# Mixture-of-experts turns: the ranks behind two fixed experts in order of size, in place of large and small in turn

## What is computed

```python
_, idx = lax.top_k(jnp.where(in_group, biased, -jnp.inf), TOP_K)      # TOP_K = 2 of 16
wts = jnp.take_along_axis(scores, idx, axis=-1)
wts = wts / wts.sum(-1, keepdims=True)
gates = jnp.einsum('tk,tke->te', wts, jax.nn.one_hot(idx, N_EXPERTS, dtype=F32)).astype(h.dtype)
y = jnp.zeros_like(x)
for e in range(N_EXPERTS):
    he = jax.nn.silu(x  wg[e]) * (x  wu[e])
    y = y + gates[:, e:e + 1] * (he  wd[e])
```

## Time and profile before

| | us |
|---|---|
| median of 3 runs | 1263.56 |
| the three runs | 1263.53, 1263.56, 1271.19 |
| the profiled execution, device time | 1273.05 |
| its span (first to last instruction) | 1270.9 |
| mean granted TensorE clock | 0.927 |
| TensorE busy (matmul) | 1055.2 (83%) |
| moved by DMA | 299.46 MB, mean 236 GB/s |

### The profile page before, as it was taken

The page is one execution under the profiler, slowest core; times in us unless marked ns, Lnnn a source line. Parts: engine busy times, 40 slices in busy tenths (PEclk is TensorE's granted clock), DMA queues, the critical chain, the costliest instruction groups (busy, mean ns, idle before and its releaser), DMA issues. The chain is left out here.

```text
span 1270.9 us, 14505 instructions
## 1 busy us (share of the span) xinstructions
PE 1055.2 (83%) x5804; PEld 615.9 (48%) x5804; DVE 346.0 (27%) x810; ACT 242.6 (19%) x542; POOL 141.3 (11%) x163
## 2 busy tenths in 40 slices
PE   4899997967898989677999867687785989998874
PEld 1344465833343434245887457577653433333333
DVE  0101125254010010123433266668236001010103
ACT  1200235121110111112333411121131101010112
POOL 1000000010000000001000056573000000000001
PEclk9999968978999999888999989899897999999988
DMA  9966840442689899992665310100060498989860
GB/s 375 428 273 265 310 180 7 143 188 103 268 367 415 371 405 388 386 426 95 225 258 207 144 46 1 67 1 1 23 242 2 166 431 344 429 348 428 342 291 33
DMA packets 22157, 299.46 MB, mean 236 GB/s; under 512 B 2560, under 2 KB 2688, under 8 KB 4032
## 3 DMA queue, kind: packets, MB, share of 16 engines
q1 hardware_dynamic: 20304, 291.34, 56.5%
q0 software_dynamic: 1776, 7.08, 1.5%
HBM read 295.27 MB, written 3.15 MB: 235 GB/s over the span
## 5 line engine op out<-in xcount | busy, mean ns | idle before, releaser
L496 PE MATMUL bank<-ring,arena 128*64 128x512 f32 x640 | 147.2, 612 | 23.0 <-DMA ring<-slots 14.3
L504 PE MATMUL bank<-ring,arena 128*32 128x512 f32 x576 | 77.0, 670 | 38.2 <-DMA ring<-slots 38.2
L496 PEld LDWEIGHTS bank<-ring,arena 128*64 128x64 f32 x640 | 46.7, 140 | 111.1 <-issue 92.1
L881 PE MATMUL bank<-act_t,ring 128*128 128x256 f32 x384 | 90.9, 392 | 8.5 <-POOLq L272 8.5
L1389 PE MATMUL bank<-ring,act_t 128*128 128x512 f32 x192 | 88.1, 614 | 3.9 <-ACTq L272 3.9
L881 PEld LDWEIGHTS bank<-act_t,ring 128*128 128x128 f32 x384 | 73.8, 197 | 22.8 <-POOLq L272 8.9
L770 DVE COPY arena<-bank 128x256 f32<-128x256 f32 x38 | 16.1, 425 | 249.9 <-PE bank L437 249.9
L539 PE MATMUL bank<-arena 64*128 64x256 f32 x608 | 76.3, 390 | 1.2 <-DVEq L433 1.2
L523 PE MATMUL bank<-ring,arena 128*64 128x512 f32 x320 | 73.1, 598 | 1.3 <-ACT arena L629 1.3
L808 POOL COPY arena<-arena 128x512 f32 (+1 forms) x38 | 19.5, 513 | 468.2 <-PE bank L496 218.3
L300 PE MATMUL bank<-ring,par 128*32 128x512 f32 x384 | 55.5, 703 | 15.6 <-DMA ring<-slots 14.5
(11 more groups left out here) (332 smaller groups left out, 1418.2 us busy)
## 6 DMA issues: line engine op xcount, KB each, us to landing
ring<-slots SPq DMA_DIRECT2D x138, 2048.0 KB, 11.8
cst<-consts SPq DMA_DIRECT2D x1, 1276.0 KB, 32.4
act_t<-x_t POOLq DMA_DIRECT2D x1, 1024.0 KB, 12.9
act_t<-state POOLq DMA_DIRECT2D x1, 1024.0 KB, 5.1
out_st<-arena POOLq DMA_DIRECT2D x4, 256.0 KB, 2.8
out_y<-arena POOLq DMA_DIRECT2D x2, 512.0 KB, 3.4
par<-params SPq DMA_DIRECT2D x1, 542.0 KB, 3.7
arena<-nat_bias POOLq DMA_DIRECT2D x1, 512.0 KB, 20.6
```

The source lines that it names most:

```text
L496: last = pe.matmul(bk[64 * t:64 * t + 64, :], x[:, 4 * m + c, 0:64], w[:, c, 512 * t:512 * t + 512], start=(m == 0 and c == 0), stop=(m == ...
L504: last = pe.matmul(bk[at:at + 32, :], x[:, 4 * m + c, 0:32], w[:, c, 512 * t:512 * t + 512], start=(m == 0 and q == 0), stop=(m == 1 and q ...
L881: last = pe.matmul(bank[i % 3][:, 0:T], w[:, c, (i % 4) * P:(i % 4 + 1) * P], act_t[:, c, :], start=(c == 0), stop=(c == KC - 1))
```

## The change

One line: the order in which the ranks take their turns. `LEAN`, `FULL`, the rows that SyncE reads and the order of all blocks follow from it. The sizes of the ranks and the work of each block stay.

```diff
 FIXED = (14, 15)
-TURNS = (0, 1, 7, 2, 8, 5, 9, 3, 10, 6, 11, 4, 12, 13, 14, 15)
+TURNS = (0, 1, 2, 3, 4, 5, 6, 7, 8, 9, 10, 11, 12, 13, 14, 15)
 LEAN_CAP = (64, 64) + (128,) * 3 + (64,) * 2 + (32,) * 9
```

## The result

| | before | changed |
|---|---|---|
| median, first comparison | 1266.02 (4 runs) | 1305.45 (3 of 4 runs) |
| ratio, 95% interval | | 1.029 (1.0225 to 1.0355) |
| median, second comparison | 1268.77 (10 runs) | 1301.72 (4 runs) |
| ratio, 95% interval | | 1.025 (1.0205 to 1.0298) |
| profiled execution, span | 1273.05, 1270.9 | 1306.7, 1304.5 |

The fourth execution of the changed kernel in the first comparison took 2651.94 us in a slow state, at a mean granted clock of 1.00, and is left out; nothing here explains it.

What follows compares the result with a forecast made beforehand. Expert loads were taken as the bound. Standstills in the wide blocks, then 27 loads at 5.03 us, lengthen the layers by 17.65 and 17.85 us; 35.5 on the median 1263.56 gives 1299, range 1288 to 1310.

Steps and rivals of the forecast that it cites:

- The bound: Expert blocks of both layers: loads set the pace, DMA engines busy for 0.94, and the stage ends with the last landing.
- The wide stretch: Eight wide blocks, steps 2 to 9: 13.27 us each, TensorE without ring waits from about 330 to 436.
- The standstills: Loads of the wide blocks: DMA engines find no free ring buffer, three times about 9 us, 33 us a layer.
- (4, 2): Down load of turn 4, a double expert: if issued at its old time, the account of held buffers is wrong.
- The landing of (6, 2): Down load of turn 6 in layer 0: issued at 423.25, lands 7.6 us later at 430.85, having found the queue empty.
- The spacing of the 27 loads behind it: Loads of turns 7 to 15: 5.03 us each, 135.8 us in all; lower bound 4.9 us a load.
- The cover and the clock: Narrow steps: down buffers come free 5.6 us before needed, so low clock of TensorE, costing 1.7 to 5.1, adds zero.
- low clock throughout: Rival: narrow steps wholly at 0.50 clock take 17.4 us against 15.1 of loads; 1336 in all, 5 in 100.
- TensorE's waits in the narrow stretch: Nine narrow experts of each layer: TensorE waits some 6 us for the loads of each.
- No change: Rival: the ring hides 20 of the 34 us by which three double experts outlast their loads; 1264, 5 in 100.
- Faster: Rival: the three earlier standstills vanish, 27 us in all, 1236; needs wide steps of 7.5 us; 3 in 100.
- The sum on the median: Whole kernel: 35.5 us for both layers added to the earlier median 1263.56, not the profiled 1273.05, gives 1299.

Runs made afterwards that it cites:

- the half-load runs: Order of before and changed order, each with expert loads of half the size in layer 1: 1229.76 us (ratio 0.9685) and 1251.16 us (ratio 0.9865).

## Why the prediction was right, point by point

**The bound.** Right. The last load sets the end of the stage, the steps behind it take what they took before (12.3 and 10.7 us), and the half-load runs show that the order costs next to nothing where loads don't bind.

**The wide stretch.** Right to the tenth. The step is 13.27 us, TensorE has no wait for the ring between 330.8 and 437, and (6, 2) is issued at 423.6 for 423.25 forecast, 92.8 us behind block 2 in both.

**The standstills.** Right in their sum, not in their places. The prediction named (4, 2) as the load that decides about its account. It was issued at 356.8 before and at 370.5 now, first before, then after:

```profile
L1746 SPq DMA_DIRECT2D ring<-slots x1: 333/333/333, 356.8 to 356.8; - x1
DMA to landing us min/median/max: 11.9/11.9/11.9
...
L1746 SPq DMA_DIRECT2D ring<-slots x1: 333/333/333, 370.5 to 370.5; - x1
DMA to landing us min/median/max: 7.6/7.6/7.6
```

Three standstills of about 9 us were to come. In layer 0 (4, 2), (5, 2) and (6, 2) land 7.4, 8.2 and 9.4 us behind their turn, and (4, 0), (5, 0) and (6, 0) are late by 2.9, 3.8 and 3.8 too, since the gate and up buffers of a double expert are held through two steps as well. The six make 35 us for the 33 of the forecast.

**The landing of (6, 2).** 9.0 us after its issue in layer 0, not 7.6, so 1.4 us too little. In layer 1 it was 7.7. The prediction says that a load into an empty queue lands after 7.6 to 7.7 us. The trace of before has 15 loads of experts that found the queue empty, and 4 of them took 8.7 to 9.8. One is (13, 2) of layer 0:

```profile
L1746 SPq DMA_DIRECT2D ring<-slots x1: 333/333/333, 509.9 to 509.9; - x1
DMA to landing us min/median/max: 9.8/9.8/9.8
```

**The spacing of the 27 loads behind it.** Mis-sized. I took 5.03 us from two stretches of before, one load now and then being 1 us late. In the narrow stretch it was (564.7 - 432.6) / 27 = 4.89 in layer 0 and (1262.9 - 1128.8) / 27 = 4.97 in layer 1. That is 3.7 and 1.7 us less than the 135.8 forecast. The bound of 4.9 from the earlier trace rows was the better row. Together with the landing, the stretches grew by 15.4 and 16.2 us, not 17.65 and 17.85: 31.6 for 35.5.

**The cover and the clock.** Right in its effect, thinner than stated. The DMA share in the narrow stretch is 1.01, so the low clock cost the loads nothing in layer 0. In layer 1 a low stretch of 10.3 us stands at 1212.5:

```profile
1212.50:1222.80 10.30, 9.46 (x44) 5.12 (x48) 0.29 (x1) 0.87 (x2) 0.40 (x1) 0.50 1.01 426
```

The `down` behind it was late, and (13, 2) was issued at 1224.8, only 8.8 us before its landing:

```profile
L1746 SPq DMA_DIRECT2D ring<-slots x1: 333/333/333, 1224.8 to 1224.8; - x1
DMA to landing us min/median/max: 8.8/8.8/8.8
```

Its turn was 8.0 us behind its issue (the load before it landed at 1227.96, and 4.9 are added). Of 5.6 us of cover, counted with 7.6 us to landing, 0.4 were left. The load took 8.8 and landed 0.7 us behind its turn. The rule quoted from the Trainium skill ("TensorE: Matmul & The Clock Gate", section "HAM oscillation — how this bites in real kernels") held in kind, since six low stretches stand in the narrow blocks of each layer, 23.9 and 34.1 us in all. The wait outlasts the compute here in the half step (2.9 us for 1.9 of matmuls) and not in the whole expert (4.3 for 8.7). It did not hold for every narrow expert, and it did not set the time. The rival "low clock throughout" (1336) fell for the reason given with it: no narrow step stayed at 0.50.

**TensorE's waits in the narrow stretch.** Some 6 us an expert were forecast. The waits of TensorE from 437 on:

```profile
PE bank L504 <- DMA ring<-slots: 38.4, 17, 2.9
```

That is 4.3 an expert. The low clock filled most of the rest: half of its 23.9 us is up to 12 us of longer matmuls, 1.3 an expert. This changes nothing at the end.

**The other rivals.** "No change" needed the ring to hide 20 of 34 us, and it hid nothing more. "Faster" needed wide steps of 7.5 us. Neither came.

**The sum on the median.** The shift was added to 1263.56. Later medians of the kernel before were 1264.3 to 1268.8, so the base was 1 to 5 us low. This and the 4 us of the terms went against each other: that 1299 came within 3 and 6 us of the two medians of the changed kernel (1301.72 and 1305.45) is in part luck. The 4 us of the stretches are the better measure of the working.

## What to carry to other kernels

When loads and an engine share a ring, compare for each piece of work the time that it holds its buffers with the time that its loads take, and follow the load whose buffer comes free last: loads behind it queue behind it, and only the last such standstill has to be worked out. Sorting by size puts all surplus of one resource at one end and all surplus of the other at the other end. Alternate them while the ring is small, and look for dead memory that can hold the one operand that is kept longest: here the buffer was worth 1.7 to 1.9%, and 2.3% together with the last double expert one turn later.

## What the runs showed of the hardware that was not expected

Executions of the kernel before differ by up to 14 us (1260.12 to 1273.84 in one set of 11), while the stretches of the changed kernel repeat within 0.4 us in its two profiles. The profiles place a good part of the difference in the attention of layer 0. Here are the sums over a low stretch of the kernel before, and then over the one at the same place in the second profile of the changed kernel:

```profile
159.30:183.20 23.90, 23.56 (x94) 15.60 (x98) 5.55 (x18) 6.43 (x25) 0.00 (x0) 0.50 0.39 154
```

```profile
166.40:176.70 10.30, 10.30 (x43) 5.74 (x41) 2.75 (x9) 3.49 (x12) 0.00 (x0) 0.50 0.08 29
```

The work is the same up to there. Block 2 starts at 330.5 in the one and at 322.4 in the other, 8.1 us apart. The low stretches differ by 13.6 us, and at half the clock that is 6.8 us of work, most of the difference. It isn't the order of the experts that does this, for the first profile of the changed kernel is like that of the kernel before, and has block 2 at 330.8:

```profile
157.80:181.70 23.90, 23.65 (x94) 15.59 (x98) 5.45 (x18) 6.34 (x24) 0.00 (x0) 0.50 0.39 156
```

In both long stretches TensorE was busy for all but 0.3 us (23.56 and 23.65 of 23.90) at 1.2 GHz, so that here a busy engine did not have its full clock. What makes the one stretch longer wasn't tried.

Single loads that land 0.4 to 1.5 us late though the queue is never empty, five to seven in a layer of the kernel before, are rare in the narrow stretch of the sorted one: none in layer 0 and three in layer 1, the late (13, 2) among them. The others come 4.9 us apart. This is the term that was mis-sized, and its cause is open.
